# Two transformer blocks of 256 tokens: coefficient pieces and modulation chunks take other places behind the steps of one feed-forward network

## The chip, the cores and the metric

The kernel runs on one core of one Trainium2 chip. The metric is the device time of one launch in microseconds (us). The program is a single launch that reads all weights from the chip's memory once and writes one output of 256 x 1024.

## What is computed

A first model of two layers (a gated delta rule with a short convolution, then a SwiGLU feed-forward network, FFN) is followed by a second model of two layers, and the change lies in that one. Cut to what matters:

```
def second_block(x, c, mod_w, mod_b, ...):
    for l in range(DEPTH):                                   # DEPTH = 2
        mod = (silu(c) @ mod_w[l] + mod_b[l]).reshape(bsz, 3, 3, D_MODEL)
        x = post_add(x, swiglu(pre(x, 0), ffn_w_in[l, 0], ffn_w_out[l, 0]), 0, 0.5)
        y = token_mixer(pre(x, 1), ..., a_re, a_im, log_dt, b_re, b_im, c_re, c_im, ...)
        x = post_add(x, y, 1, 1.0)
        x = post_add(x, swiglu(pre(x, 2), ffn_w_in[l, 1], ffn_w_out[l, 1]), 2, 0.5)

def swiglu(h, w_in, w_out):                                  # 1024 -> 2 x 2816 -> 1024
    gate, up = split(h @ w_in)
    return (silu(gate) * up) @ w_out
```

The mixer holds a state-space recurrence in parallel to attention. Its coefficients (`lam_bar = exp(lam * dt)`, `b_bar`, and tables of sines and cosines for each step of time) depend on weights alone, and not on the tokens, so they can be made at any time ahead of the mixer. So can `mod`, a product of a single vector with a matrix of 1024 x 9216 per layer.

## The kernel before

**Steps.** The program is a list of steps (`STEPS`), each a tuple of block, layer, kind and index. All five engines walk the same list, each in its own loop, and take from each step the instructions that are theirs. An engine executes strictly in the order of its own loop; it is held by semaphores where another engine has to be done. So a place in the list is a place in every engine's queue.

**The FFN.** It has 33 steps, numbered 0 to 32 here: `gu` (22 times: a 128-wide slice of gate and up, 48 matmuls of 256 columns into a bank `stream`) and `down` (11 times: two slices of the product back to 1024, 24 matmuls of 512 columns into `works`). The order is `gu, gu`, and then eleven times `gu, down, gu`, so that steps 3, 6, 9, ... 30 and 32 are `down`; the last group has no `gu` left. Behind a `gu`, ACT computes a tanh of the gate (line 1046), DVE makes `hid` from it (lines 1411 and 1413), ACT rounds `hid` to `g_hi` (line 896) and POOL makes the remainder `g_lo` (line 1621).

**Weights.** Each step reads one chunk of 1 MB from memory (two units of 128 x 1024). SP issues the loads in the order of the steps into a ring of four places (`raw`, `RAWS = 4`). ACT rounds a unit to `w_hi` (line 866), DVE computes the remainder `w_lo = raw - w_hi` (line 1143), and PE multiplies with both (three matmuls for each product, lines 453 to 455 and 467 to 469). `w_hi` and `w_lo` have four slots, which is two steps: a slot is written when PE is done with the unit four before it. Ahead of a step, ACT and DVE prepare the units of that step and of the next; PE begins a unit when its `w_lo` is there.

**Pieces between the steps.** A `mod` step multiplies one chunk of the modulation matrix with a vector: two instructions on DVE of 128 x 1024 (line 1252) and 1 MB to load. Most of these chunks have a ring of their own (`side`); the eight of numbers 40 to 47, which stand in the FFN ahead of the second model's mixer in layer 0, go through the ring of the weights. There SP waits before it loads into a place until DVE is done with what stood there:

```
                if c >= RAWS:
                    kind, n = chunks[c - RAWS]
                    if kind == "mod":
                        sp.wait_ge(s_mod_used, 2 * n)
                    else:
                        sp.wait_ge(s_lo_ready, n)
                sp.dma_start(raw[:, c % RAWS, :], w[at]).then_inc(loaded[c % RAWS], 16)
```

The coefficients of the mixer are 17 pieces in the list `COEFS`: `coef 0` to `coef 6` on DVE (with a few instructions on ACT in `coef 0` and `coef 2`), `table 0` to `table 7` (an even one makes arguments on DVE; an odd one reduces them on DVE, lines 1513 and 1514, and lets ACT take the sine, line 1070), `kzero` (32 small matmuls and four copies on ACT) and `bzero` (eight transposes and two copies on ACT). They stand in the same FFN, in both layers; layer 1 has no modulation chunks there. `mod`, `coef`, `table`, `kzero` and `bzero` are `FILLERS`: ahead of one, ACT and DVE first prepare the units of the two steps that follow.

Before the change, one coefficient piece stands ahead of each of the steps 8 to 24, and `behind_ffn` spreads the eight modulation chunks over the steps from 6 on, which puts them behind steps 8, 11, 14, 17, 20, 23, 26 and 28. A chunk behind step k stands ahead of the coefficient piece of step k + 1.

Of the kernel before, what the change touches and what calls it, by code (L numbers as in the profile page):

```python
# [45 lines left out]
FILLERS = ("mod", "coef", "table", "kzero", "bzero")  # L46
SLOTS = 4

COEFS = [("coef", 0), ("coef", 1), ("coef", 2), ("coef", 3), ("coef", 4), ("table", 0), ("table", 1), ("coef", 5),
         ("coef", 6), ("table", 2), ("kzero", 0), ("table", 3), ("bzero", 0), ("table", 4), ("table", 5), ("table", 6),  # L50
         ("table", 7)]
BLK = T // 2


def ffn_order():

    out = [("gu", 0), ("gu", 1)]
    for j in range(FT // 2):
        if 2 * j + 2 < FT:
            out.append(("gu", 2 * j + 2))  # L60
        out.append(("down", j))
        if 2 * j + 3 < FT:
            out.append(("gu", 2 * j + 3))
    return out
# [32 lines left out]
    ("glu", 5), ("hsplit", 3), ("glu", 6), ("glu", 7)]  # L97

SECOND = (
    [("pre", 0)] + ffn_order()[:8] + [("grow", 0)]  # L100
    + [s for i, step in enumerate(ffn_order()[8:8 + len(COEFS)]) for s in (COEFS[i], step)]
    + ffn_order()[8 + len(COEFS):]
    + [("post", 0), ("pre", 1)] + MIXER
    + [("aout", j) for j in range(4)] + [("grow", 1)]
    + [("mout", j) for j in range(DT // 2)] + [("post", 1), ("pre", 2)]
# [4 lines left out]
FFN_STEPS = len(ffn_order())  # L110


def behind_ffn(steps, which, mods):

    places = [k for k, s in enumerate(steps) if s[2] in ("gu", "down")][which * FFN_STEPS + 6:(which + 1) * FFN_STEPS - 4]
    out, done = [], 0
    for k, s in enumerate(steps):
        out.append(s)
        if k in places:
            upto = len(mods) * (places.index(k) + 1) // len(places)  # L120
            out += mods[done:upto]
            done = upto
    return out


def first_block(L):
    return [(1, L, kind, i) for kind, i in FIRST if (kind, L) not in (("crow", 1), ("grow", 0))]


def second_block(L):  # L130
    return [(2, L, kind, i) for kind, i in SECOND]


MODS = [[(1 + layer, 0, "mod", i) for i in range(MODT // 2)] + [(1 + layer, 0, "modsum", 0), (2, layer, "mods", 0)] for layer in range(LAYERS)]
STEPS = behind_ffn(first_block(0), 0, MODS[0][:20]) + behind_ffn(first_block(1), 0, MODS[0][20:] + MODS[1][:4]) + \
        [(1, LAYERS - 1, "final", 0)] + \
        behind_ffn(behind_ffn(second_block(0), 0, MODS[1][4:12]), 1, MODS[1][12:]) + second_block(1)
SIDE_OF = {m: k for k, m in enumerate([m for m in range(MODT) if not 40 <= m < 48])}
UNITS_OF = {"lead": 1, "pair": 2, "out": 1, "mout": 2, "gu": 2, "down": 2, "aout": 1, "glu": 1}

# [54 lines left out]
def build(nc, w, x_in, const_in, p1_in, p2_in, bt_in, out):  # L195
    with ExitStack() as ctx:
# [52 lines left out]
        def p2_(L, name, lo=0, hi=None):  # L249
            return view(par2[:], P2, name, lo, hi)  # L250

        xs = mx[:, 0:TT * D].rearrange("p (a n) -> p a n", a=TT)
        grow = mx[:, TT * D:TT * D + D]
# [113 lines left out]
        for B, L, kind, i, n in NUMBERED:  # L367
# [5 lines left out]
            else:  # L373
                for v in range(n["split"], n["split"] + units_of(B, kind, i)):
                    if v % 2 == 0:
                        loads.append(("raw", len(chunks)))
                        chunks.append(("split", v + 2))
        chunk_of_unit = [c for c, (kind, _) in enumerate(chunks) if kind == "split" for _ in range(2)]
        chunk_of_mod = {n - 1: c for c, (kind, n) in enumerate(chunks) if kind == "mod"}
        mod_of_side = {k: m for m, k in SIDE_OF.items()}  # L380
# [746 lines left out]
        def _(dve):  # L1127
# [3 lines left out]
            def link(ins):  # L1131
                links[0] += 1
                ins.then_inc(s_dve_self, 1)
                dve.wait_ge(s_dve_self, links[0])
# [39 lines left out]
            for B, L, kind, i, n in NUMBERED:  # L1174
# [66 lines left out]
                elif kind == "mod":  # L1241
                    dve.wait_ge(s_crow_done, 2)
                    if n["mod"] in SIDE_OF:
                        k = SIDE_OF[n["mod"]]
# [227 lines left out]
                elif kind == "coef":  # L1472
# [4 lines left out]
                    if i == 4:  # L1477
                        v.memset(Bx["k0"], 0.0).then_inc(s_k0_zero, 1)
                        cre, cim = (by_state(p2_(L, k)) for k in ("c_re", "c_im"))
                        TTn(cp[:, 0, 0], cre, wide(t["kr"]), ALU.mult)  # L1480
                        link(TTn(t0, cim, wide(t["ki"]), ALU.mult))
                        TTn(cp[:, 0, 1], cre, wide(t["ki"]), ALU.mult)
                        link(TTn(t1, cim, wide(t["kr"]), ALU.mult))
                        TTn(cp[:, 0, 0], cp[:, 0, 0], t0, ALU.subtract)
                        STT(cp[:, 0, 1], cp[:, 0, 1], -1.0, t1, ALU.mult, ALU.subtract).then_inc(s_cre_done, 1)
                        dve.wait_ge(s_cre_done, L + 1)
                    elif i == 5:
                        TTn(cp[:, 1, 0], cp[:, 0, 0], wide(t["lr"]), ALU.mult)
                        link(TTn(t0, cp[:, 0, 1], wide(t["li"]), ALU.mult))
                        TTn(cp[:, 1, 1], cp[:, 0, 1], wide(t["lr"]), ALU.mult)  # L1490
                        link(TTn(t1, cp[:, 0, 0], wide(t["li"]), ALU.mult))
                        TTn(cp[:, 1, 0], cp[:, 1, 0], t0, ALU.add)
                        link(TTn(cp[:, 1, 1], cp[:, 1, 1], t1, ALU.subtract))
                    else:
                        dve.wait_ge(bt_ld, 16 * (L + 1))
                        bre, bim = (by_state(bt[:, e, :]) for e in range(2))
                        o0, o1 = (by_state(b0t[:, e, :]) for e in range(2))
                        TTn(o0, bre, wide(t["lr"]), ALU.mult)
                        link(TTn(t0, bim, wide(t["li"]), ALU.mult))
                        TTn(o1, bre, wide(t["li"]), ALU.mult)  # L1500
                        link(TTn(t1, bim, wide(t["lr"]), ALU.mult))
                        link(TTn(o0, o0, t0, ALU.subtract))
                        TTn(o1, o1, t1, ALU.add).then_inc(s_b0t_done, 1)
                        dve.wait_ge(s_b0t_done, L + 1)
# [11 lines left out]
                elif kind == "fwd":  # L1516
                    k = 4 * L + i
# [10 lines left out]
                elif kind == "rec":  # L1528
                    k = 4 * L + i
# [7 lines left out]
                elif kind == "back":  # L1537
                    k = 4 * L + i
# [248 lines left out]
```

## Time and profile before

| what | value |
|---|---|
| time, median of 3 runs | 2066.39 us (2064.84 to 2066.61) |
| profiled execution | 2071.73 us, span 2069.9 us |
| PE busy | 1944.0 us, 94% of the span |
| DVE busy | 1468.3 us, 71% |
| ACT busy | 984.2 us, 48% |
| POOL busy | 235.5 us, 11% |
| chain that ended last | PE 77%, DVE 13%, ACT 4%, issue 4%, DMA 1% |
| first FFN of the second model, layer 0 | about 799 to 1008 us |
| the same FFN in layer 1 | about 1450 to 1640 us |

The table is read from the top down: the share of an engine says how full it is over the whole span, and the chain says which engine's work followed upon which up to the end. The shares are averages over stages of different kinds; the two FFNs that the change touches are 400 us of the 2070. The span is the time between the first and the last instruction of the profiled execution, whose own time is 1.8 us longer; the median of the runs without the profiler is 5.3 us below that.

### The profile page before, as it was taken

Reading aid. Unit: us, or ns where it says so; the run is one execution under the profiler, and the core shown is the slowest. Engines: PE = TensorE matmul, PEld = TensorE weight load, DVE = VectorE, ACT = ScalarE, POOL = GpSimd, SP = SyncE. Lnnn points to the kernel's source line nnn. Section 1 sums busy time; section 2 is a strip of 40 time slices with the busy share of each in tenths; the row PEclk is TensorE's granted clock in tenths of the full one; section 3 lists DMA queues with packets and bytes.
Section 4 is the critical chain, followed back from the end, with each engine's and each line's share of the span. In section 5 each row is a group of like instructions: output and inputs, shape, how many; then the busy total and the mean of one; then the engine's idle time right before and its main releaser. Section 6 shows DMA issues by size and latency. Waiting matters only on the chain.

```text
span 2069.9 us, 34524 instructions
## 1 busy us (share of the span) xinstructions
PE 1944.0 (94%) x14256; PEld 1819.6 (88%) x14256; DVE 1468.3 (71%) x2235; ACT 984.2 (48%) x1563; POOL 235.5 (11%) x182
## 2 busy tenths in 40 slices
PE   6899999999999998989899989998999899999998
PEld 6898899898989997888798879997989798888997
DVE  5655699866577986787677676998587667676555
ACT  5434544454454445454534454445456444455443
POOL 0210111112001111111000001111111100001111
PEclk9999999999999999999899999999999899999999
DMA  5223698332259864455433347894545433253552
GB/s 218 92 103 122 253 339 344 142 123 82 82 187 356 331 248 149 161 218 204 171 125 121 127 160 306 352 353 149 182 167 177 157 123 123 102 183 126 182 184 100
DMA packets 53293, 384.27 MB, mean 186 GB/s; under 512 B 5904, under 2 KB 6032, under 8 KB 6928
## 3 DMA queue, kind: packets, MB, share of 16 engines
q1 hardware_dynamic: 53136, 382.05, 49.4%
q8 instruction: 113, 1.85, 0.4%
q14 instruction: 44, 0.36, 0.0%
HBM read 380.98 MB, written 1.05 MB: 185 GB/s over the span
## 4 chain that ended last, share of the span: by engine, by line
PE 77%; DVE 13%; ACT 4%; issue 4%; DMA 1%; DVEq 0%; SPq 0%; ACTq 0%
PE stream L453 15%; PE stream L454 15%; PE stream L455 15%; PE works L467 5%; PE works L468 5%; PE works L469 5%; DVE w_lo L1143 3%; ACT w_hi L866 2%; DVE mx L1252 2%; DMA raw<-w 1%; PE stream L509 1%; PE stream L510 1%; PE stream L511 1%; PE works L788 1%; DVE x L1232 1%
## 5 line engine op out<-in xcount | busy, mean ns | idle before, releaser
L453 PE MATMUL stream<-h_hi,w_hi 128*128 128x256 f32 x2976 | 858.3, 288 | 16.0 <-DVE w_lo L1143 15.9
L1143 DVE TENSOR_TENSOR w_lo<-raw,w_hi 128x1024 fp32r<-128x1024 f32 x572 | 738.0, 1307 | 187.9 <-ACT w_hi L866 161.6
L454 PE MATMUL stream<-h_lo,w_hi 128*128 128x256 f32 x2976 | 850.9, 286 | 0.0
L455 PE MATMUL stream<-h_hi,w_lo 128*128 128x256 f32 x2976 | 850.3, 286 | 0.0
L866 ACT ACTIVATE w_hi<-raw 128x1024 fp32r<-128x1024 f32 x572 | 591.7, 1051 | 130.7 <-PE works L469 82.0
L453 PEld LDWEIGHTS stream<-h_hi,w_hi 128*128 128x128 f32 x2976 | 580.1, 195 | 23.7 <-issue 20.6
L454 PEld LDWEIGHTS stream<-h_lo,w_hi 128*128 128x128 f32 x2976 | 580.1, 195 | 2.1
L455 PEld LDWEIGHTS stream<-h_hi,w_lo 128*128 128x128 f32 x2976 | 579.6, 195 | 0.0
L1621 POOL TENSOR_TENSOR g_lo<-hid,g_hi 128x256 fp32r<-128x256 f32 x140 | 191.0, 1366 | 1612.3 <-ACT g_hi L896 1612.3
L1046 ACT ACTIVATE gate_t<-stream 128x256 f32<-128x256 f32 x132 | 50.6, 383 | 407.1 <-PE stream L455 404.4
L467 PE MATMUL works<-w_hi,g_hi 128*128 128x512 f32 x528 | 207.5, 393 | 3.8 <-DVE w_lo L1143 3.8
L468 PE MATMUL works<-w_hi,g_lo 128*128 128x512 f32 x528 | 206.3, 391 | 0.0
L469 PE MATMUL works<-w_lo,g_hi 128*128 128x512 f32 x528 | 205.5, 389 | 0.0
L1411 DVE SCALAR_TENSOR_TENSOR gate_t<-gate_t,stream 128x256 f32<-128x256 f32 x132 | 55.3, 419 | 196.1 <-ACT gate_t L1046 192.0
L1252 DVE CUSTOM_DVE_ANT_0 mx<-mx,crow 128x1024 f32<-128x1024 f32 x128 | 150.8, 1213 | 0.0
L467 PEld LDWEIGHTS works<-w_hi,g_hi 128*128 128x128 f32 x528 | 99.3, 188 | 26.0 <-issue 4.5
L469 PEld LDWEIGHTS works<-w_lo,g_hi 128*128 128x128 f32 x528 | 99.1, 188 | 21.1
L468 PEld LDWEIGHTS works<-w_hi,g_lo 128*128 128x128 f32 x528 | 99.4, 188 | 18.0
L896 ACT ACTIVATE g_hi<-hid 128x256 fp32r<-128x256 f32 x140 | 58.2, 418 | 68.6 <-DVE hid L1413 59.0
L892 ACT ACTIVATE h_hi<-hf 128x256 fp32r<-128x256 f32 x112 | 45.1, 415 | 67.2 <-DVE hf L1206 27.4
L576 PE MATMUL stat<-con,mx 128*128 128x128 f32 x32 | 10.5, 432 | 57.5 <-DVE mx L1195 57.5
L509 PE MATMUL stream<-h_hi,w_hi 128*128 128x256 f32 x160 | 52.6, 329 | 11.3 <-DVE h_lo L1151 11.3
(407 smaller groups left out, 2159.2 us busy)
## 6 DMA issues: line engine op xcount, KB each, us to landing
raw<-w SPq DMA_DIRECT2D x294, 1024.0 KB, 4.8
mx<-w SPq DMA_DIRECT2D x64, 1024.0 KB, 7.0
par<-p_in SPq DMA_DIRECT2D x2, 1110.0 KB, 7.1
x<-x_in SPq DMA_DIRECT2D x1, 1024.0 KB, 6.9
mx<-bt_in SPq DMA_DIRECT2D x2, 512.0 KB, 5.9
out<-x SPq DMA_DIRECT2D x4, 256.0 KB, 2.4
con<-const_in SPq DMA_DIRECT2D x1, 968.0 KB, 4.9
par<-p_in SPq DMA_DIRECT2D x1, 225.0 KB, 7.0
```

The costliest lines, as they stand in the source:

```text
L453: mm(o, hi, r_hi[:, kt, :], start=first, stop=False, skip_group_check=True)
L454: mm(o, hi, r_lo[:, kt, :], start=False, stop=False, skip_group_check=True)
L455: last = mm(o, lo, r_hi[:, kt, :], start=False, stop=end, skip_group_check=True)
L467: mm(sums[q][:], a_hi, hi, start=first, stop=False)
L468: mm(sums[q][:], a_lo, hi, start=False, stop=False)
L469: last = mm(sums[q][:], a_hi, lo, start=False, stop=end)
L509: mm(o, hi, h_hi[:, kt, :], start=k == 0 and e == 0, stop=False, skip_group_check=True)
L866: f(w_hi[:, v % SLOTS, :], raw[:, chunk_of_unit[v] % RAWS, (v % 2) * UNIT:(v % 2 + 1) * UNIT], ACT.Copy).then_inc(s_hi_ready, 1)
L896: f(g_hi[:, slot, :], hid[:, g % 2, :], ACT.Copy).then_inc(s_ghi_done, 1)
L1143: v.tensor_tensor(w_lo[:, q % SLOTS, :], raw[:, chunk_of_unit[q] % RAWS, (q % 2) * UNIT:(q % 2 + 1) * UNIT], w_hi[:, q % SLOTS, :].bitcast ...
L1252: v.tensor_tensor_reduce(rows, rows, crow[:], 1.0, 0.0, ALU.mult, ALU.add, modacc[:, 2 * i + e:2 * i + e + 1]).then_inc(s_mod_used, 1)
L1621: v.tensor_tensor(g_lo[:, slot, :], hid[:, g % 2, :], g_hi[:, slot, :].bitcast(F32), ALU.subtract)\
```

## The change

The coefficient list has 20 pieces where it had 17: `coef 4`, `coef 5` and `coef 6` are each cut in two (now 4 and 5, 6 and 7, 8 and 9) without a change to their instructions. The pieces stand behind the steps 3, 4, 5, 7, 8, 9, 11, ... 28, which leaves out each fourth one. The eight modulation chunks of layer 0 stand behind steps 2, 6, 10, ... 30, so that no step has both behind it. The gain row (`grow`) stays behind step 7. Layer 1 gets the same coefficient places, with no chunks. Also `table 1` to `table 4` change their places relative to `coef` pieces, `kzero` stands behind step 16 (it stood ahead of 18) and `bzero` behind step 24 (it stood ahead of 20).

```
-COEFS = [("coef", 0), ("coef", 1), ("coef", 2), ("coef", 3), ("coef", 4), ("table", 0), ("table", 1), ("coef", 5),
-         ("coef", 6), ("table", 2), ("kzero", 0), ("table", 3), ("bzero", 0), ("table", 4), ("table", 5), ("table", 6),
-         ("table", 7)]
+COEFS = [("coef", 0), ("coef", 1), ("coef", 2), ("coef", 3), ("coef", 4), ("table", 0), ("coef", 5), ("table", 1),
+         ("coef", 6), ("coef", 7), ("kzero", 0), ("table", 2), ("coef", 8), ("table", 3), ("coef", 9), ("table", 4),
+         ("bzero", 0), ("table", 5), ("table", 6), ("table", 7)]
+RAW_MODS = {2 + 4 * k: k for k in range(8)}
+COEF_STEPS = [k for k in range(3, 29) if k not in RAW_MODS]
...
 SECOND = (
-    [("pre", 0)] + ffn_order()[:8] + [("grow", 0)]
-    + [s for i, step in enumerate(ffn_order()[8:8 + len(COEFS)]) for s in (COEFS[i], step)]
-    + ffn_order()[8 + len(COEFS):]
+    [("pre", 0)]
+    + [s for k, step in enumerate(ffn_order()) for s in
+       [step] + [("grow", 0)] * (k == 7) + [c for at, c in zip(COEF_STEPS, COEFS) if at == k]]
...
+def behind_steps(steps, which, mods, at):
+
+    ffn = [k for k, s in enumerate(steps) if s[2] in ("gu", "down")][which * FFN_STEPS:(which + 1) * FFN_STEPS]
+    out = []
+    for k, s in enumerate(steps):
+        out.append(s)
+        if k in ffn and ffn.index(k) in at:
+            out.append(mods[at[ffn.index(k)]])
+    return out
...
-        behind_ffn(behind_ffn(second_block(0), 0, MODS[1][4:12]), 1, MODS[1][12:]) + second_block(1)
+        behind_ffn(behind_steps(second_block(0), 0, MODS[1][4:12], RAW_MODS), 1, MODS[1][12:]) + second_block(1)
...
                         link(TTn(t1, cim, wide(t["kr"]), ALU.mult))
+                    elif i == 5:
                         TTn(cp[:, 0, 0], cp[:, 0, 0], t0, ALU.subtract)
```

Two places on DVE show what this does. The first is in layer 0, from the preparation of weights behind step 11 on; lines 1252 are a modulation chunk, 1478 to 1485 are `coef 4`. Before:

```order
L1143 TENSOR_TENSOR w_lo<-raw,w_hi 128x1024 x2
L1252 ISA raw,modacc<-raw,crow 128x1024
L1252 ISA modacc 128x1
L1252 ISA raw,modacc<-raw,crow 128x1024
L1252 ISA modacc 128x1
L1478 MEMSET mx 128x512
L1480 TENSOR_TENSOR mx<-par,mx 128x512
L1481 TENSOR_TENSOR mx<-par,mx 128x512
L1482 TENSOR_TENSOR mx<-par,mx 128x512
L1483 TENSOR_TENSOR mx<-par,mx 128x512
L1484 TENSOR_TENSOR mx<-mx 128x512
L1485 SCALAR_TENSOR_TENSOR mx<-mx 128x512
```

In the changed kernel `coef 4` stands behind step 8. Its lines are 1491 to 1496; 1526 and 1527 are `table 0`, 1424 and 1426 the two instructions on `gate_t` and `hid` of a `gu`:

```order
L1424 SCALAR_TENSOR_TENSOR gate_t<-gate_t,stream 128x256
L1426 SCALAR_TENSOR_TENSOR hid<-gate_t,stream 128x256
L1156 TENSOR_TENSOR w_lo<-raw,w_hi 128x1024 x2
L1491 MEMSET mx 128x512
L1493 TENSOR_TENSOR mx<-par,mx 128x512
L1494 TENSOR_TENSOR mx<-par,mx 128x512
L1495 TENSOR_TENSOR mx<-par,mx 128x512
L1496 TENSOR_TENSOR mx<-par,mx 128x512
L1156 TENSOR_TENSOR w_lo<-raw,w_hi 128x1024 x2
L1526 TENSOR_TENSOR mx<-con,mx 128x512
L1527 TENSOR_SCALAR mx<-mx 128x512
L1424 SCALAR_TENSOR_TENSOR gate_t<-gate_t,stream 128x256
```

The modulation chunk is gone from ahead of it, and its last two instructions have moved to a piece of their own.

The second place is the next heavy one: before, behind step 14, a chunk and `coef 5` (lines 1488 to 1493) in a row:

```order
L1143 TENSOR_TENSOR w_lo<-raw,w_hi 128x1024 x2
L1252 ISA raw,modacc<-raw,crow 128x1024
L1252 ISA modacc 128x1
L1252 ISA raw,modacc<-raw,crow 128x1024
L1252 ISA modacc 128x1
L1488 TENSOR_TENSOR mx<-mx 128x512
L1489 TENSOR_TENSOR mx<-mx 128x512
L1490 TENSOR_TENSOR mx<-mx 128x512
L1491 TENSOR_TENSOR mx<-mx 128x512
L1492 TENSOR_TENSOR mx<-mx 128x512
L1493 TENSOR_TENSOR mx<-mx 128x512
L1143 TENSOR_TENSOR w_lo<-raw,w_hi 128x1024 x2
```

Now the first four of these (lines 1502 to 1505) stand behind step 13, and the chunk (line 1265) behind step 14:

```order
L1156 TENSOR_TENSOR w_lo<-raw,w_hi 128x1024 x2
L1502 TENSOR_TENSOR mx<-mx 128x512
L1503 TENSOR_TENSOR mx<-mx 128x512
L1504 TENSOR_TENSOR mx<-mx 128x512
L1505 TENSOR_TENSOR mx<-mx 128x512
L1424 SCALAR_TENSOR_TENSOR gate_t<-gate_t,stream 128x256
L1426 SCALAR_TENSOR_TENSOR hid<-gate_t,stream 128x256
L1156 TENSOR_TENSOR w_lo<-raw,w_hi 128x1024 x2
L1265 ISA raw,modacc<-raw,crow 128x1024
L1265 ISA modacc 128x1
L1265 ISA raw,modacc<-raw,crow 128x1024
L1265 ISA modacc 128x1
```

Between the two stand the gate of a `gu` and the preparation of the next weights.

## Rows read from the trace of the kernel before

**Rows 1.** The page: the span, then the chain that ended last, by engine.

```profile
span 2069.9 us, 34524 instructions
...
PE 77%; DVE 13%; ACT 4%; issue 4%; DMA 1%; DVEq 0%; SPq 0%; ACTq 0%
```

**Rows 2.** Four FFNs, busy time by stretch: changed one in layers 0, 1; third; last.

```profile
core 0: us, PE busy (x) PEld busy (x) DVE busy (x) ACT busy (x) POOL busy (x), PEclk, DMA share, GB/s
799.00:1008.00 209.00, 194.01 (x1376) 181.27 (x1376) 152.52 (x212) 104.33 (x139) 31.01 (x22) 0.97 0.53 204
1449.70:1640.40 190.70, 187.63 (x1385) 176.20 (x1385) 133.96 (x178) 103.83 (x138) 30.96 (x22) 1.00 0.51 180
1244.70:1433.00 188.30, 186.56 (x1314) 174.79 (x1314) 160.20 (x213) 83.86 (x114) 30.24 (x22) 1.00 0.80 313
1876.00:2061.50 185.50, 185.49 (x1313) 174.76 (x1312) 103.82 (x110) 84.64 (x116) 30.96 (x22) 1.00 0.45 159
```

**Rows 3.** POOL in order of time: first and last `g_lo` of the last FFN.

```profile
1881.50 1.44 POOL L1621 TENSOR_TENSOR g_lo<-hid,g_hi 128x256 fp32r<-128x256 f32 x1 [90.01 <-ACT g_hi L896]
...
2058.83 0.74 POOL L1621 TENSOR_TENSOR g_lo<-hid,g_hi 128x256 fp32r<-128x256 f32 x1 [9.79 <-ACT g_hi L896]
```

**Rows 4.** Waits in 843 to 1008 us, longest sum first (us, times, longest).

```profile
ACT w_hi L866 <- DMA raw<-w: 26.5, 8, 8.7
...
PE stream L453 <- DVE w_lo L1143: 13.0, 6, 3.6
```

**Rows 5.** Groups on DVE in 799 to 1008 us (busy, mean ns, idle before).

```profile
L1143 DVE TENSOR_TENSOR w_lo<-raw,w_hi 128x1024 fp32r<-128x1024 f32 x66 | 87.7, 1343 | 23.8 <-ACT w_hi L866 19.9
L1252 DVE CUSTOM_DVE_ANT_0 raw<-raw,crow 128x1024 f32<-128x1024 f32 x16 | 18.9, 1213 | 0.0
```

**Rows 6.** DVE in order of time: behind step 11, layer 0, with the odd table.

```profile
873.56 1.21 DVE L1252 CUSTOM_DVE_ANT_0 raw<-raw,crow 128x1024 f32<-128x1024 f32 x1
...
875.99 0.48 DVE L1478 MEMSET mx<- 128x512 f32 x1
...
878.97 0.69 DVE L1484 TENSOR_TENSOR mx<-mx 128x512 f32<-128x512 f32 x1
...
880.30 2.36 DVE L1143 TENSOR_TENSOR w_lo<-raw,w_hi 128x1024 fp32r<-128x1024 f32 x2
882.58 0.69 DVE L1510 TENSOR_TENSOR mx<-con,mx 128x512 f32<-128x512 f32 x1
...
883.76 0.42 DVE L1411 SCALAR_TENSOR_TENSOR gate_t<-gate_t,stream 128x256 f32<-128x256 f32 x1
...
887.60 0.68 DVE L1513 TENSOR_SCALAR mx<-mx 128x1024 f32<-128x1024 f32 x1
888.32 1.23 DVE L1514 TENSOR_TENSOR mx<-mx 128x1024 f32<-128x1024 f32 x1
892.47 0.42 DVE L1411 SCALAR_TENSOR_TENSOR gate_t<-gate_t,stream 128x256 f32<-128x256 f32 x1 [2.92 <-ACT gate_t L1046]
```

**Rows 7.** ACT in order of time: gate of step 8; then the first odd table.

```profile
849.07 0.38 ACT L1046 ACTIVATE gate_t<-stream 128x256 f32<-128x256 f32 x1 [3.68 <-PE stream L455]
...
889.58 1.06 ACT L1070 ACTIVATE mx<-mx 128x1024 f32<-128x1024 f32 x1 [2.24 <-DVE mx L1514]
890.66 1.28 ACT L1046 ACT_TABLE_LOAD   x1
891.95 0.38 ACT L1046 ACTIVATE gate_t<-stream 128x256 f32<-128x256 f32 x1
```

**Rows 8.** DVE behind step 8: weights prepared, then the modulation chunk.

```profile
850.61 2.91 DVE L1143 TENSOR_TENSOR w_lo<-raw,w_hi 128x1024 fp32r<-128x1024 f32 x2
853.45 1.21 DVE L1252 CUSTOM_DVE_ANT_0 raw<-raw,crow 128x1024 f32<-128x1024 f32 x1
```

**Rows 9.** PE in layer 1: the starts that it waited for.

```profile
1541.44 0.36 PE L453 MATMUL stream<-h_hi,w_hi 128*128 128x256 f32 x1 [1.60 <-DVE w_lo L1143]
```

**Rows 10.** The loads of weights issued in 843 to 1008 us, issue to landing.

```profile
DMA to landing us min/median/max: 4.7/7.4/10.7
```

**Rows 11.** SP and ACT behind step 26: three loads issued, and the first used.

```profile
977.67 1.28 SPq L424 DMA_DIRECT2D raw<-w  x3
...
982.36 2.00 ACT L866 ACTIVATE w_hi<-raw 128x1024 fp32r<-128x1024 f32 x2 [8.65 <-DMA raw<-w]
```

More of the change, by code:

```diff
@@ L1486, in _ @@
                         dve.wait_ge(s_cre_done, L + 1)
-                    elif i == 5:
+                    elif i == 6:
                         TTn(cp[:, 1, 0], cp[:, 0, 0], wide(t["lr"]), ALU.mult)
@@ L1491, in _ @@
                         link(TTn(t1, cp[:, 0, 0], wide(t["li"]), ALU.mult))
+                    elif i == 7:
                         TTn(cp[:, 1, 0], cp[:, 1, 0], t0, ALU.add)
                         link(TTn(cp[:, 1, 1], cp[:, 1, 1], t1, ALU.subtract))
-                    else:
+                    elif i == 8:
                         dve.wait_ge(bt_ld, 16 * (L + 1))
@@ L1501, in _ @@
                         link(TTn(t1, bim, wide(t["lr"]), ALU.mult))
+                    else:
                         link(TTn(o0, o0, t0, ALU.subtract))
```

## Prediction

> **What bounds the kernel now.** I read the page first: PE is at work 94% of the span and holds 77% of the chain that ended last, DVE 13% [rows 1]. So time can only come back where PE waits or where its clock is low. The windows by stage show where that is. Four FFNs of the second model do the same matrix work. The last one has nothing between its steps: 185.50 us, PE busy for 185.49 of them. The third has 24 modulation chunks through the ring of their own, and it loses 1.7 us (188.30 against 186.56 busy). The one that is changed takes 190.70 in layer 1 with PE busy for 187.63, and 209.00 in layer 0 with PE busy for 194.01, the granted clock there being 0.97 of full speed and not 1.00 [rows 2].
>
> From these rows comes the most that the change can give. The small matmuls of `kzero` and `bzero` and the rest that both layers share put PE's busy time at 187.63. In layer 0 PE is idle for 209.00 - 194.01 = 15.0 us, and its own work takes 194.01 - 187.63 = 6.4 us longer at the lower clock: 21.4 us. In layer 1 it is idle for 190.70 - 187.63 = 3.1 us, at full clock. Together 24.5 us.
>
> Next, whom PE waits for. The waits name `w_lo` on DVE, and behind it ACT, which waits 26.5 us in eight pieces for weights from memory [rows 4]. So there are two shortages, DVE's time and the ring of four chunks, and the ring itself waits for DVE, since a place with a modulation chunk is free only when DVE has multiplied it.
>
> **DVE's account.** PE's pace from the first to the last `g_lo` of the undisturbed FFN is (2058.83 - 1881.50) / 31 = 5.7 us per step [rows 3]. DVE's plain work is 103.82 / 33 = 3.15 us per step; the coefficients cost 133.96 - 103.82 = 30.1 us, and the eight chunks 152.52 - 133.96 = 18.6 us, 2.3 each [rows 2] (two instructions of 1.21 [rows 5]). At an odd table DVE also stands idle for 2.92 us: ACT cannot take the sine before DVE has the arguments, then loads the table of the tanh for 1.28 us, and only then makes the tanh of the next gate, for which DVE waits [rows 6, 7]. Four of them are 11.7 us.
>
> Before, steps 8 to 24 hold all coefficients and six chunks: 17 x 3.15 + 30.1 + 6 x 2.3 + 11.7 = 109.2 us of DVE in 17 x 5.7 = 96.9 us of PE. DVE is 12.3 us short. After, the same pieces stand behind steps 3 to 28, also with six chunks: 26 x 3.15 + 30.1 + 13.8 + 11.7 = 137.5 us in 26 x 5.7 = 148.2 us. DVE has 10.7 us to spare, at 93%. No instruction is added or removed; three more list places find the weights that they would prepare already asked for. The three cuts cost nothing: what is cut is followed by a weights preparation that would have come anyway.
>
> **The lumps.** An average that fits can still stall. After the tanh of a `gu` (849.07 [rows 7]) DVE is done with the next weights at 853.5, 4.5 us later [rows 8]. The next gate comes at 5.7 + 0.5. So 1.7 us of a piece are free, and another 2.4 us only delay the first unit of the weights two steps on (ready 3.0 us after the tanh, wanted 5.4 us after it). A piece of up to 4.1 us between two `gu` costs PE nothing. Before, the chunk and `coef 4` run from 873.56 to 880.3, 6.7 us in a row [rows 6], and so it goes on behind step 14. After, the longest piece is the first part of `coef 4`, 878.97 - 875.99 = 3.0 us, and the chunk is 2.4.
>
> I carried DVE's lateness from step to step with these numbers. In layer 0 PE waits 0.3 us ahead of the weights behind step 14, 0.7 behind 25 and 1.7 behind 28, where an odd table stands between two `gu`: 2.7 us. In layer 1 it is 1.4. The same walk over layer 1 of before gives 5.0 us where the trace has 3.1, the first of the waits being 1.60 [rows 9]; it exaggerates, and I scale by 3.1 / 5.0: 1.7 and 0.9 us.
>
> On the table switch the row decides: the load takes 1.28 us and the tanh starts 0.01 us behind it [rows 7]. The Trainium skill (ScalarE: Activation LUTs, What ACT_TABLE_LOAD costs) adds a drain of about 1.38 us to each switch; the trace does not show it here. As a mechanism, 1.4 us more at each odd table would add about 4 us of idle PE in layer 0 and 3 in layer 1 and put the time near 2057; the rows of before leave it a chance of 0.01.
>
> **The ring.** The eight chunks stand at a distance of three steps before, so between a chunk and the weights of four steps on there is a further chunk in SP's order, 1 MB that is loaded first. After, the distance is four: the load that waits for a chunk is at once the weights of the step four on. A chunk behind a `gu` is done 4.5 + 2.4 = 6.9 us after the tanh; ACT and DVE then need 1.0 [rows 11] and 1.45 us (half of 2.91 [rows 8]) for the first unit, and PE wants it 3 x 5.7 - 0.3 = 16.8 us after the tanh. So 7.4 us are left for the load, which is just the median of this stretch (4.7 to 10.7) [rows 10]. Behind steps 14 and 26 DVE is about 2.5 us late when it comes to the chunk. There a load of 7.4 us is 2.5 late and one of 4.7 us is not; behind step 26 of before three loads went out together and the first was in use 4.7 us later [rows 11]. I take half, 1.25 us at each of the two: 2.5 us.
>
> By the Trainium skill (DMA: Bandwidth & Descriptors, under its cost components, 2.0 us fixed plus bytes over 436 GB/s) a chunk lands after an estimated 4.4 us. The ring would then cost nothing and the time would be about 2045. The median row speaks against that, the shortest for it; this case lies inside my forecast.
>
> **The sum.** Idle PE left in layer 0: 1.7 + 2.5 = 4.2 us. The lower clock cost 6.4 us beside 15.0 us of idleness, 0.43 for each, and in layer 1 nothing beside 3.1; I take 0.43 x 4.2 = 1.8. Layer 1 keeps 0.9. That leaves 6.9 of the 24.5 us, a gain of 17.6. The profiled execution (2071.7 us around a span of 2069.9) would become 2054.1, and the median of the runs, 5.3 us below it, 2066.4 - 17.6 = 2048.8 us. Moves without a price: the load of `bt` goes one chunk later in SP's order, with ten steps until `kzero`; `coef 0` to `coef 3` now stand between steps 3 and 8, where DVE had 2.5 us free per step; the last chunk, behind step 30, delays only weights that are wanted two steps later. If that cover is gone, each costs its own 1 to 2.5 us.
>
> **The rivals.** First, the ring stays a bound: DVE's shortage of 12.3 us goes, and what else layer 0 loses, 21.4 - 12.3 = 9.1, stays, because DVE at 93% is late at most chunks and loads take the median or more. With 2.2 from layer 1 the gain is 14.5 less the 1.7 of the lumps: about 2053.6, up to 2060. For it speaks that ACT waited longer for memory than for anything else; against it that these waits came when chunks were late, which they are less now. Chance 0.20.
>
> Second, slower: the chunks now sit directly in front of the weights four places on, and every one of the eight holds PE up. At the longest landing, 10.7 us, the first unit is there 6.9 + 10.7 + 2.5 = 20.1 us after the tanh, 3.3 late; with the clock 4.7 us, and eight times that is 37.8, less 24.5: 13 us slower, 2079.7. It decides from a landing of 9.5 us on (24.5 / 8 / 1.43 = 2.1 late). Single loads reached this, the median is 7.4, and three of the eight stand behind a `down`, where DVE need not wait for a gate. Chance 0.04.
>
> Third, no change: PE's waits come from the odd tables' handshake and from the clock, which the change leaves alone, or a new wait early in the FFN, at steps 2 to 8 that run without one now, takes all back. The rows of layer 1, with the same tables and a loss of only 3.1, speak against it. Within 4 us of 2066.4: chance 0.04.
>
> **How the numbers follow.** The forecast has 0.71: 2042 (all 24.5) to 2055 (twice the 6.9 left), at 2048.8. With 0.01 for the table drain, 0.20, 0.04 and 0.04 that is 1. A range of 2042 to 2058 holds the forecast's case and most of the first rival's, some 0.85. What a measurement of this kernel can tell from no change is about 0.2%, 4 us. Faster by more has 0.92, within it 0.04, slower 0.04.
>
> **What would show it.** In the changed profile the FFN of layer 0 should take about 194 us with PE idle for 4 and a granted clock of 0.99, that of layer 1 about 188.5; DVE's busy time in both is the same as before. ACT's waits for memory should fall from 26.5 to under 8 us, and no DVE piece behind a `gu` be longer than 3 us. Waits of PE at steps 14, 26 and 29 would confirm the lumps; waits three or four steps behind each chunk, the first rival. The prediction is wrong if PE waits appear ahead of step 8, or if the loads take 9 us or more.

## The result, and the profile after

The changed kernel takes 2052.7 us (median of 4 runs, 2046.41 to 2054.02); the kernel before, 2065.6 us over the runs beside it. The ratio is 0.9928, with a 95% interval of 0.9906 to 0.9951: about 15 us less, 10 to 19 (the two medians are 12.9 us apart). In five further rounds it was 0.9929 (0.9906 to 0.9953).

The windows of the changed kernel, for the changed FFN in layers 0 and 1 and the last FFN, answer to [rows 2]:

```profile
core 0: us, PE busy (x) PEld busy (x) DVE busy (x) ACT busy (x) POOL busy (x), PEclk, DMA share, GB/s
796.80:987.60 190.80, 186.99 (x1376) 174.95 (x1376) 151.94 (x212) 103.79 (x139) 31.01 (x22) 1.00 0.54 213
1430.50:1619.30 188.80, 187.93 (x1386) 176.30 (x1385) 133.77 (x178) 104.04 (x138) 30.92 (x22) 1.00 0.50 182
...
1856.80:2042.30 185.50, 185.49 (x1313) 174.76 (x1313) 103.86 (x110) 84.71 (x116) 30.94 (x22) 1.00 0.45 159
```

Layer 0 went from 209.0 to 190.8 us. PE is idle for 3.8 of them instead of 15.0, and works at full clock. Layer 1 went from 190.7 to 188.8. DVE's busy time is within 0.6 us of that before in both, and the last FFN is unchanged. Together that is 20.1 us; the two spans differ by 19.1, of which 2.1 are already there at the first `g_lo` of the program, ahead of all that the change touches, and 3.3 are lost again in stages behind the two FFNs (last section).

The waits in layer 0's stretch (796 to 988 us), on PE and on ACT, answer to [rows 4]:

```profile
PE stream L466 <- DVE w_lo L1156: 3.8, 3, 2.7
...
ACT w_hi L879 <- DMA raw<-w: 12.2, 7, 2.8
```

And these are the starts of PE that waited, three in layer 0 and two in layer 1, in order of time:

```profile
886.98 0.36 PE L466 MATMUL stream<-h_hi,w_hi 128*128 128x256 f32 x1 [0.71 <-DVE w_lo L1156]
957.41 0.35 PE L466 MATMUL stream<-h_hi,w_hi 128*128 128x256 f32 x1 [0.43 <-DVE w_lo L1156]
977.29 0.36 PE L466 MATMUL stream<-h_hi,w_hi 128*128 128x256 f32 x1 [2.67 <-DVE w_lo L1156]
...
1590.82 0.36 PE L466 MATMUL stream<-h_hi,w_hi 128*128 128x256 f32 x1 [0.43 <-DVE w_lo L1156]
1608.46 0.36 PE L466 MATMUL stream<-h_hi,w_hi 128*128 128x256 f32 x1 [0.43 <-DVE w_lo L1156]
```

Counted at PE's pace they stand ahead of steps 16, 28 and 31, and in layer 1 ahead of 28 and 31: each two steps behind a gate that came late on DVE, those of 14, 26 and 29.

### The profile page after: what moved, and what is told of

The parts are those of the page before. It is cut to its first block, busy times and chain, and to the rows that moved or that the text cites. A ratio compares the mean times of both kernels' runs of the same rounds, so it can differ in the third digit from the quotient of the medians.

```text
span 2050.8 us, 34530 instructions
## 1 busy us (share of the span) xinstructions
PE 1938.4 (95%) x14256; PEld 1814.3 (88%) x14256; DVE 1467.6 (72%) x2235; ACT 983.8 (48%) x1563; POOL 235.3 (11%) x182
## 4 chain that ended last, share of the span: by engine, by line
PE 80%; DVE 11%; ACT 4%; issue 3%; DMA 1%; DVEq 0%; SPq 0%; ACTq 0%
PE stream L466 16%; PE stream L467 16%; PE stream L468 16%; PE works L480 5%; PE works L481 5%; PE works L482 5%; DVE w_lo L1156 2%; ACT w_hi L879 2%; DVE mx L1265 2%; PE stream L522 1%; PE stream L523 1%; PE stream L524 1%; PE works L801 1%; DMA raw<-w 1%; DVE x L1245 1%
## 5 line engine op out<-in xcount | busy, mean ns | idle before, releaser
L466 PEld LDWEIGHTS stream<-h_hi,w_hi 128*128 128x128 f32 x2976 | 577.5, 194 | 12.8 <-issue 9.6
```

The lines of the kernel that those rows point to most:

```text
L466: mm(o, hi, r_hi[:, kt, :], start=first, stop=False, skip_group_check=True)
```

## The experiments

For all of them I compare the length of an FFN from its first to its last `g_lo` in the order of time on POOL, because it is short and repeats: the last FFN, which no edit touches, takes 177.3 us in nine of the fourteen profiles and 176.7 in the other five. Each length is read from one profile of its kernel; the changed kernel's two differ by 0.3 us in layer 0. Before, it is 1005.48 - 804.34 = 201.1 us in layer 0 and 1637.85 - 1455.12 = 182.7 in layer 1.

| kernel | layer 0, us | layer 1, us | whole kernel, ratio to before |
|---|---|---|---|
| before | 201.1 | 182.7 | 1 |
| changed | 183.1 | 180.5 | 0.9928 (0.9906 to 0.9951) |
| changed, again | 182.8 | 180.5 | 0.9929 (0.9906 to 0.9953) |
| chunks_only | 189.8 | 182.7 | 0.9959 (0.9943 to 0.9975) |
| coefs_only | 201.7 | 180.5 | 1.0014 (0.9995 to 1.0032) |
| joined | 187.3 | 181.6 | 0.9935 (0.9908 to 0.9962) |
| apart3 | 201.6 | 180.1 | 0.9995 (0.9972 to 1.0017) |
| weights_first | 182.7 | 180.1 | 0.9920 (0.9894 to 0.9947) |
| ring_alone | 185.2 | 182.2 | one run |
| product_alone | 191.4 | 182.8 | one run |
| neither | 182.5 | 182.7 | one run |
| spread_ring_alone | 187.4 | 180.5 | one run |
| spread_product_alone | 189.3 | 179.9 | one run |
| sine_later | 178.6 | 179.2 | 0.9862 (0.9831 to 0.9893) |

**One half of the change at a time.** For chunks_only the kernel before gets the new places of the chunks:

```
-        behind_ffn(behind_ffn(second_block(0), 0, MODS[1][4:12]), 1, MODS[1][12:]) + second_block(1)
+        behind_ffn(behind_steps(second_block(0), 0, MODS[1][4:12], RAW_MODS), 1, MODS[1][12:]) + second_block(1)
```

> Only the eight modulation chunks move (behind 2, 6, ... 30); the 17 coefficient pieces stay ahead of steps 8 to 24. Lengths are from the first to the last g_lo of the FFN; before 201.1 us in layer 0 and 182.7 in layer 1, changed kernel 183.1 and 180.5. Theory DVE (the loss was DVE's shortage in steps 8 to 24 and the ring only followed): four chunks instead of six fall into the full stretch, 4.6 of 12.3 us are relieved, and chunks still meet heavy pieces at 10, 14, 18 and 22: layer 0 takes 192 to 196 us. Theory ring (the distance of three steps between chunks is the loss): 185 to 188 us. Layer 1 stays at 182.7 with both.

coefs_only is the changed kernel with that line turned back:

> Only the coefficient pieces are cut and spread (20 behind steps 3 to 28); the chunks stay behind steps 8, 11, 14, 17, 20, 23, 26 and 28, so that seven of the eight share a step with a piece. Theory DVE: DVE has enough time again, with lumps of at most 2.4 + 3.0 = 5.4 us: layer 0 takes 185 to 190 us against 201.1. Theory ring: the distance of three stays and with it most of the loss, 194 us or more. Layer 1 goes to 180.5 with both.

The chunks alone give 11.4 of the 18 us in layer 0 (189.8, better than the DVE theory's 192 to 196 and short of the ring theory's 185 to 188). The coefficients alone give none: 201.7, where the DVE theory had 185 to 190. In coefs_only DVE has the same instructions as in the changed kernel, the pieces over the same steps (all eight chunks lie within steps 8 to 28, though, where the changed kernel has five), and yet stands idle for 24.9 us waiting for ACT, which waits for memory (798 to 1008 us):

```profile
DVE w_lo L1156 <- ACT w_hi L879: 24.9, 10, 6.0
ACT w_hi L879 <- DMA raw<-w: 24.8, 7, 8.8
```

So DVE's shortage over steps 8 to 24, the first half of my account, does not by itself hold layer 0 at 201. In layer 1, where there are no chunks, spreading does give its 2.2 us, and with the chunks at a distance of four it gives 189.8 - 183.1 = 6.7.

**Which part of a chunk costs: its product on DVE or its place in the ring.** Both are variants of the kernel before. In ring_alone the product is narrow:

```
-                        rows = piece[:, e * UNIT:(e + 1) * UNIT]
-                        v.tensor_tensor_reduce(rows, rows, crow[:], 1.0, ...)
+                        wide_ = UNIT if n["mod"] in SIDE_OF else 8
+                        rows = piece[:, e * UNIT:e * UNIT + wide_]
+                        v.tensor_tensor_reduce(rows, rows, crow[:, 0:wide_], 1.0, ...)
```

> Kernel before, but DVE multiplies only 8 of the 1024 columns of each half of the eight chunks 40 to 47 (their sums are left out); the loads, their places in the ring and the waits stay. Layer 0's FFN, 201.1 us before. Theory DVE: without 18 us of DVE work the chunks cost nothing, and the length is that of layer 1, 182.7, to 185 us. Theory ring: the loads still stand in each other's way, 192 us or more.

In product_alone the chunk is left out of the ring:

```
             elif kind == "mod":
-                loads.append(("raw", len(chunks)))
-                chunks.append(("mod", n["mod"] + 1))
+                loads.append(("none", n["mod"]))
```

> Kernel before, but the eight chunks 40 to 47 are not loaded and take no place in the ring; DVE does instructions of the same size at the same places on a vector that lies there (these sums of the modulation are left out). Theory DVE: most of the loss stays, 193 to 199 us. Theory ring: it is gone, 183 to 187 us. The share of the ring is what is missing to 201.1.

The third kernel, neither, makes both edits:

> Kernel before without the loads of the eight chunks and with 8 columns of product each (their sums are left out). Both theories: layer 0 like layer 1, 182 to 184 us. It is the floor for the two kernels that keep one of the two.

Each of the three was executed once. Against the floor of 182.5 us the loads alone cost 2.7, the products alone 8.9, and both 18.6. The sum of the parts is 11.6; 7 us come only from the two together. The same two edits on coefs_only, with the spread coefficients, show it too:

> coefs_only (spread pieces, chunks at distance three, 201.7 us) with DVE multiplying only 8 columns of each half of the eight chunks (their sums are left out); loads and waits stay. If the distance of the loads alone is the loss, above 192 us. If it needs the late chunks that DVE's work makes, as before (185.2 us with the same cut there), 181 to 185 us.

> coefs_only without the loads of the eight chunks, DVE doing instructions of the same size at the same places on a vector that lies there (these sums are left out). With the average of DVE's time as the cause, nothing of the 201.7 us should be left in this kernel beyond the lumps of 5.4 us: 184 to 188 us. If the lumps alone explain the 201.7, it stays above 195.

187.4 and 189.3 us, against 201.7 with both; layer 1 of these kernels, which has no chunks at all, is at 180. The loads as the sole cause had above 192 us in the first, and the lumps as the sole cause above 195 in the second; neither held. The other two expectations (181 to 185 and 184 to 188) were nearer and missed as well, by 2.4 and 1.3 us. Most of the loss needs both, a chunk that is finished late and a load that waits for it.

**Sharing a step, or the distance.** apart3 keeps the old places of the chunks (as in coefs_only) and the cut pieces, and keeps them apart:

```
-COEF_STEPS = [k for k in range(3, 29) if k not in RAW_MODS]
+COEF_STEPS = [k for k in range(3, 31) if k not in (8, 11, 14, 17, 20, 23, 26, 28)]
```

> Coefficients cut in 20 as in the changed kernel, chunks at their old distance of three (behind 8, 11, 14, ... 28), but no step has both: the pieces take the 20 steps from 3 to 30 that have no chunk. coefs_only, in which they share steps, took 201.7 us in layer 0, the changed kernel 183.1. If what hurts is that a chunk and a piece share a step, it is 183 to 187 us. If it is the distance of three, which puts the load of the next chunk ahead of the weights that wait for this one, it is 192 us or more, with ACT's waits for memory above 15 us.

201.6 us, so sharing a step is not what costs. What the distance of three does is seen in the trace at the chunk behind step 14. In apart3, on DVE, SP and ACT:

```profile
892.41 1.22 DVE L1265 CUSTOM_DVE_ANT_0 raw<-raw,crow 128x1024 f32<-128x1024 f32 x1
...
893.66 1.28 SPq L437 DMA_DIRECT2D raw<-w  x3
...
901.13 1.06 ACT L879 ACTIVATE w_hi<-raw 128x1024 fp32r<-128x1024 f32 x1 [4.92 <-DMA raw<-w]
```

And in the changed kernel:

```profile
889.58 1.22 DVE L1265 CUSTOM_DVE_ANT_0 raw<-raw,crow 128x1024 f32<-128x1024 f32 x1
...
890.83 2.60 SPq L437 DMA_DIRECT2D raw<-w  x4
...
895.63 1.06 ACT L879 ACTIVATE w_hi<-raw 128x1024 fp32r<-128x1024 f32 x1 [2.25 <-DMA raw<-w]
```

In both, SP issues a batch of three loads 0.03 us after the chunk's product ends, since all of it was queued behind that one wait (the fourth load of the changed kernel's row left 2.3 us later, behind a wait of its own). In the changed kernel the first load of the batch is the weights of step 18, and ACT uses them 4.8 us after the issue. At distance three the first load is the next chunk; the weights of step 18 are second, and ACT has them 7.5 us after the batch began. Their own place had been free since step 15's `w_lo` was made, which ended at 884.86:

```profile
881.96 2.90 DVE L1156 TENSOR_TENSOR w_lo<-raw,w_hi 128x1024 fp32r<-128x1024 f32 x2 [0.45 <-ACT w_hi L879]
```

So they left about 9 us later than their own place allowed, because SP takes its loads in order and stood at the one that waited for the chunk. DVE waits for ACT, and the next chunk's product stands behind DVE's work on those weights, so that it is late too and releases the next batch late: a loop of product, load, rounding, product. At PE's pace it has 17.2 us (three steps) at distance three and 22.9 at four. In apart3 the product behind step 14 ends 20.1 us after the one behind 11 (873.56 to 893.63), and the one behind 17 again 17.6 us later.

**The order of the loads alone.** weights_first is apart3 with each of the eight chunks loaded one place later. Nothing moves on PE, DVE or ACT:

```
             elif kind == "mod":
-                loads.append(("raw", len(chunks)))
-                chunks.append(("mod", n["mod"] + 1))
+                held.append((n["mod"] + 1, len(loads) + len(held)))
...
+                        for m, source in held:
+                            loads.append(("raw", len(chunks), source))
+                            chunks.append(("mod", m))
+                        held = []
```

> apart3 (chunks at distance three, 201.6 us in layer 0's FFN, ratio 0.9995) with one change on SP alone: the load of each of the eight chunks goes out one load later, behind the weights of the step that follows it, so that weights no longer stand behind a chunk's load in the batch that a finished chunk releases. All steps on PE, DVE and ACT stay as they are. If the order of the loads (1 MB ahead of the weights, about 2.7 us, in a loop that three steps leave no room for) is the cause of the 201.6, the FFN falls to 183 to 188 us and ACT's waits for memory from 27.8 to under 10 us, ratio 0.990 to 0.994. If it is the amount, a chunk every three steps, 196 us or more.

182.7 us from 201.6, ratio 0.9920. In its waits (797 to 989 us) ACT's wait for memory is gone from the list, 27.8 us in apart3, and what is left of DVE's waits for ACT and of all of PE's is this:

```profile
DVE w_lo L1159 <- ACT w_hi L882: 3.9, 4, 1.4
PE works L483 <- POOL g_lo L1640: 3.2, 1, 3.2
PE stream L469 <- DVE w_lo L1159: 0.3, 1, 0.3
```

The 3.2 us lie ahead of step 32, behind the last `g_lo` and so outside the measured length; apart3 has 4.4 us at the same place. Over the whole stretch weights_first takes 190.60 us with PE busy for 187.09, which is the changed kernel's 190.80 within 0.2. The weights of step 18 leave ahead of the chunk's product, and ACT finds them there:

```profile
883.48 0.33 SPq L440 DMA_DIRECT2D raw<-w  x1
...
891.01 1.21 DVE L1268 CUSTOM_DVE_ANT_0 raw<-raw,crow 128x1024 f32<-128x1024 f32 x1
...
894.72 1.05 ACT L882 ACTIVATE w_hi<-raw 128x1024 fp32r<-128x1024 f32 x1
```

So the edit did more than exchange two loads within a batch: it took the next weights out of the batch, and the weights of step 19, which are in it behind a chunk, are wanted a step later. It settles the cause: the weights that are wanted next stood in SP's order behind a load that waited for a chunk's product. The amount of loads and DVE's work are those of apart3. With eight loads in another order, chunks every three steps do as well as every four. Whether an exchange within the batch alone would do was not tried.

**The cuts.** joined is the changed kernel with the three cut pieces whole:

```
+PLACE = {("coef", 5): 8, ("coef", 7): 13, ("coef", 9): 19}
...
-       [step] + [("grow", 0)] * (k == 7) + [c for at, c in zip(COEF_STEPS, COEFS) if at == k]]
+       [step] + [("grow", 0)] * (k == 7) + [c for at, c in zip(COEF_STEPS, COEFS) if PLACE.get(c, at) == k]]
```

> The changed kernel, but with the three cut pieces whole again (coef 5 directly behind coef 4, 7 behind 6, 9 behind 8), at 4.0 to 4.3 us each; all other places stay. If the size of a lump matters beside the average, the two behind steps 13 and 19 pass what is free: layer 0 takes 184.5 to 187 us against 183.1, layer 1 181 to 182 against 180.5. If only the average over the stretch counts, both stay within 0.5 us of the changed kernel.

Layer 0 takes 187.3 us, 4.2 more than with the cuts and a little above the range; layer 1 1.1 more, as expected. The size of a lump matters beside the average. The ratio of the whole kernel, 0.9935, cannot be told from the changed one's: the mixer stages were shorter in that profile by the same amount, as the last section shows.

**The size of the gain.**

> The changed kernel once more, for the size of the gain: the profiles differ by 19.1 us of span and the medians by 12.9. If the profiled execution of before was a long one and the gain of the runs is what counts, the ratio is 0.992 to 0.994. If the gain is what the two FFNs give (18.2 + 1.9 us), it is 0.990 to 0.991.

0.9929, the first of the two. The profile of before was one of its longer executions (2071.7 us; 24 runs of it beside these kernels went from 2056.6 to 2074.2, median 2066.9).

**What is left.** sine_later puts each sine of an odd table behind the next step, as one more kind of piece between steps:

```
+SINES = {13: 0, 21: 1, 26: 2, 29: 3}
...
+       + [("sine", SINES.get(k))] * (k in SINES)]
...
-                elif kind == "table" and i % 2:
-                    act.wait_ge(s_tab_arg, 4 * L + i // 2 + 1)
-                    f(tabs[i // 2], tabs[i // 2], ACT.Sin, scale=6.2831850).then_inc(s_tab_sin, 1)
+                elif kind == "sine":
+                    act.wait_ge(s_tab_arg, 4 * L + i + 1)
+                    f(tabs[i], tabs[i], ACT.Sin, scale=6.2831850).then_inc(s_tab_sin, 1)
```

> The changed kernel, with the sine of each odd table taken from its piece and put behind the next step as a step of its own on ACT, so that ACT no longer waits for DVE's arguments ahead of a gate. If the handshake of the odd tables is what is left of the waits (0.7, 0.4 and 2.7 us in layer 0, 0.4 and 0.4 in layer 1), PE's idle time in the two FFNs falls from 4.7 to 0 to 2 us and the time by 3 to 4 us. If what is left is the late chunk behind step 26 and its load, the 2.7 us stay, and at most 1 us is gained.

PE no longer waits for `w_lo` in either FFN. The windows of layers 0 and 1 in sine_later are full:

```profile
797.00:983.50 186.50, 186.47 (x1377) 175.37 (x1376) 152.28 (x212) 104.42 (x139) 31.05 (x22) 1.00 0.55 218
1424.30:1611.40 187.10, 187.09 (x1382) 176.05 (x1382) 133.98 (x177) 103.80 (x137) 30.96 (x22) 1.00 0.52 183
```

So without the handshake nothing is left, also of the 2.67 us behind the table at step 28. That does not make the handshake their only part. Ahead of that table the load behind the chunk of step 26 was late too, in the changed kernel:

```profile
966.12 1.06 ACT L879 ACTIVATE w_hi<-raw 128x1024 fp32r<-128x1024 f32 x1 [2.30 <-DMA raw<-w]
967.21 2.90 DVE L1156 TENSOR_TENSOR w_lo<-raw,w_hi 128x1024 fp32r<-128x1024 f32 x2 [1.74 <-ACT w_hi L879]
```

The table's arguments follow on DVE directly behind, so the two delays stand in a row, and no run takes this load's away alone. The two FFNs give 182.8 - 178.6 + 180.5 - 179.2 = 5.5 us against the changed kernel's repetition, more than the 3 to 4 expected and more than the 4.4 us for which PE waited there; the rest is not explained. The ratio of 0.9862 is a gain of 14 us over the changed kernel, and most of that does not come from the edit's own places. It is the fastest kernel here.

## Why the prediction was right, and where not

**The bound and the most to gain.** 24.5 us in the two FFNs; 20.1 came. The forecast was 17.6 us, 2048.8; the median is 2052.7, the interval 10 to 19 us. The whole time alone does not speak for the forecast: the first rival, the ring as a bound, had 2053.6, which is nearer. What speaks for the forecast is where the time went. Layer 0's stretch takes 190.8 us (forecast 194) and layer 1's 188.8 (188.5), 20.1 us less together, where that rival had 12.8. That 2052.7 lies so near 2053.6 is chance: the FFNs gave 2.5 us more than forecast, the mixer stages took 3.3 back, and the profile of before, from which the rows are, was longer than most of its runs.

**The walk of the lumps** named the right late gates, 14, 26 and 29, and put PE's waits one to two steps too early. It had 0.3, 0.7 and 1.7 us behind steps 14, 25 and 28; the trace has 0.71, 0.43 and 2.67 ahead of steps 16, 28 and 31, where the delayed weights are used. Layer 1: 0.9 forecast, 0.9 measured, after a scaling by 3.1 / 5.0 that layer 0 did not bear out (3.8 us there, 2.7 before scaling and 1.7 after). joined and sine_later confirm the two ingredients, the size of a piece and the handshake of the odd tables.

**Idle PE in layer 0** was 4.2 us in the forecast and 3.8 in the trace, and the agreement is in part luck. The 4.2 were 1.7 for the lumps and 2.5 for the ring, 1.25 behind each of the steps 14 and 26. The late loads are in the trace at both places (2.25 and 2.30 us on ACT), but the first (at 895.63) is followed by no wait of PE until 957.41, the 0.71 us at 886.98 being ahead of it, and behind the second the load's delay and the table's are in a row; the trace does not say how the 2.67 us divide between the two terms.

**DVE's account failed as an explanation.** The prediction put 12.3 of the 21.4 us down to DVE being short in steps 8 to 24, and by it coefs_only was expected at 185 to 190 us. It stayed at 201.7. The busy times were added up rightly, but DVE's idle time, 24.9 us there, was not spare time: it stood waiting for weights whose loads stood behind a chunk's. The step "the ring" of the prediction described that order correctly (a further chunk, 1 MB, loaded first) and priced it too low: at 2.5 us for what stays, and in the first rival at the 9.1 us that DVE's shortage left over. The loads, the products and the distance form one loop, and no split into two addends describes it: 2.7 and 8.9 us alone, 18.6 together. As I read it, the time was forecast well all the same because the change removes DVE's crowding and the chunk ahead of the weights at once, so that the division between them did not enter the sum.

**The clock.** I had 1.8 us of lower clock left in layer 0; there was none (186.99 us busy against 187.93 in layer 1, granted clock 1.00 and not 0.99). PE's longest wait there was 2.7 us.

**ACT's waits for memory** were to fall below 8 us and fell to 12.2. Few of them reach PE: sine_later still has 7.3 us of them and PE busy for 186.47 of 186.50 us, and weights_first has none. Of the signs of being wrong, neither came: no PE wait ahead of step 8, and the loads of the changed kernel's stretch (796 to 988 us) took this long:

```profile
DMA to landing us min/median/max: 4.7/7.1/11.3
```

The median of the same stretch before is 7.0, and even the shortest is above the 4.4 us that the prediction worked out from the Trainium skill (DMA: Bandwidth & Descriptors, the cost components); that section is on transfers that GpSimd issues, and SP issues these.

**The table switch.** The trace of the changed kernel again has the tanh right behind its table load, as in [rows 7], at all four odd tables of layer 0; the last is

```profile
973.09 1.28 ACT L1059 ACT_TABLE_LOAD   x1
974.38 0.38 ACT L1059 ACTIVATE gate_t<-stream 128x256 f32<-128x256 f32 x1
```

The drain that the Trainium skill (ScalarE: Activation LUTs, What ACT_TABLE_LOAD costs) adds would have put PE's idle time near 8 us, and it is 3.8.

**What was not in the prediction:** that stages outside the change would move. Behind the changed FFNs, the mixer stages took 245.7 and 245.9 us in the changed kernel, where they took 244.7 and 243.7 before; 3.3 us of the gain went back there.

## What to carry to other kernels

In a ring that several kinds of loads share in program order, look at what one late consumer releases: everything queued behind its wait goes out as one batch, also loads whose own places have long been free. Put what the critical engine needs next ahead of the load that waits; the wrong order cost here 19 us of 201, and the right one takes no instruction more. And an engine's idle time beside a shared queue isn't slack until you have named what it waits for: take the load away and the work away, one at a time and together, before adding up shortages.

## What the runs showed of the hardware

The same instructions of a mixer stage take between 239.3 and 246.1 us from the last `g_lo` of the FFN ahead to the first of the one behind, in the fourteen profiles of this study, whose kernels do not differ there. PE's idle time in these stretches is 17.7 to 20.2 us, its busy time 219.6 to 227.7, at a mean granted clock of 0.97 to 0.92. So most of the difference is the granted clock. The changed kernel and sine_later, layer 1, the first 40 us and the rest of that stretch:

```profile
1616.40:1656.40 40.00, 32.16 (x202) 29.95 (x201) 22.87 (x47) 21.16 (x44) 0.74 (x1) 0.74 0.23 83
1656.40:1862.30 205.90, 194.73 (x1510) 176.37 (x1509) 147.87 (x264) 94.14 (x172) 2.87 (x4) 0.97 0.35 126
```

```profile
1608.40:1648.40 40.00, 31.81 (x237) 29.80 (x236) 27.08 (x53) 22.68 (x45) 0.74 (x1) 0.87 0.23 79
1648.40:1847.70 199.30, 187.79 (x1480) 169.67 (x1479) 143.62 (x258) 92.64 (x170) 2.90 (x5) 0.99 0.36 128
```

PE's granted clock is 0.74 behind the FFN in the one and 0.87 in the other (a mean: in slices of 4 us it goes between 1.00, which is 2.4 GHz, and 0.50, which is 1.2), and its busy time over the whole stretch is 226.9 against 219.6 us. PE has just been idle in parts there, between the FFN and the mixer: in both kernels it does nothing from 4 to 8 us behind the start of these windows, and the clock is at 0.50 in one of the next slices. The lengths come back: 245.7 and 245.9 us in the changed kernel, 245.9 and 246.0 in its repetition. What selects the stretches of low clock was not tried. Between two kernels of this study it is worth up to 6.8 us in one stage, in either direction, against the 15 us that the change gives, and 9.3 of the 15.5 us between the spans of sine_later (2035.5) and of the changed kernel's repetition (2051.0) come from the two mixer stages. Whether sine_later keeps them after the next edit is open.
